# Gated DeltaNet scan: decays and write strengths spread over the partitions by DMA instead of by products with ones

## The chip, the cores and the metric

The program runs on one core of one Trainium2 chip. The metric is the device time of one execution in microseconds (us); lower is better. Engines are named as in the profile: PE is TensorE (PEld its weight loads), DVE VectorE, ACT ScalarE, POOL GpSimd, SP SyncE, which here only issues DMAs.

## What is computed

Two layers of a hybrid diffusion backbone over 1024 latent and 256 context tokens, width 1024, all in float32. Layer 0 has a bidirectional gated DeltaNet of 4 heads, then a mixture of experts (MoE); layer 1 has windowed attention, then an MoE. The change lies in the DeltaNet scan alone. For each direction, head and chunk of tokens the reference has

```
g = jnp.cumsum(to_chunks(log_a), axis=-1)
decay = jnp.exp(jnp.where(incl, g[..., :, None] - g[..., None, :], -jnp.inf))
a_mat = jnp.where(strict, jnp.einsum('nbhid,nbhjd->nbhij', kb, kc) * decay, 0.0)
t_mat = lax.linalg.triangular_solve(eye + a_mat, ...)
qk = jnp.where(incl, jnp.einsum('nbhid,nbhjd->nbhij', qc, kc) * decay, 0.0)
q_dec = qc * jnp.exp(g)[..., None]
def step(s, inp):
    v_new = uc - wc @ s;  o = qd @ s + qkc @ v_new;  s = s * gl + kd^T @ v_new
```

(the three products of `step` are written shortened). `kb` is k times the write strength beta. The difference g_i - g_j needs g once along the partitions (a column, which the kernel has) and once along the free axis, the same on every partition (a row). So does beta. This "row on every partition" of g and of beta is what the change makes in another way.

## The kernel before

The kernel is a chain of stages; an all-engine barrier stands before each, and each engine has its own hand-written program in a stage. `delta_scan` is one stage. It takes chunks of 128 tokens, so there are NT = 10 steps; in step s direction 0 (forward) works on tile s and direction 1 (backward) on its own tile. Both directions, written d0 and d1 here, are interleaved on every engine, and a [128, 4, 128] buffer holds the four heads. Steps 0 and 1 are unrolled, the other eight run in a loop of two steps a pass (`u` is the parity). State `S` is carried from step to step, so a step's last instructions feed the next step's.

One step, in the order of the work:

- POOL multiplies a triangle by log_a (`GU`, L806) and the identity by beta (`BI`, L807) for d0, then for d1, and signals `rows_in`.
- PE multiplies each with a matrix of ones (L967, L968): bank 0 then holds the row of g on all partitions, bank 1 that of beta. Then `g_rows` is signalled. Behind them in PE's queue are K^T K and K^T Q (L958).
- ACT takes exp of bank 0 (`EG`, L852), DVE subtracts the column of g (`Dc`, L894), clips at 0 (L895), ACT takes exp (L855), POOL masks it with the triangle (`Dm`, L811).
- DVE: `DB` = decay x beta row (L900), `AT` = DB x K^T K (L902), `KQ` = Dm x K^T Q (L904), for d0 and then d1. I call the two instances of a line its d0 and d1 instance.
- PE turns AT (L980), DVE makes T (L907, L908) while POOL makes TT (L815, L817); six merge levels invert (1 + A): on each PE makes P (`heads(bank[d][1], AT[d], T[d])`), DVE `Pm` (L912), PE two products, DVE two subtractions (L923, L925).
- The tail: products with S, R (L928, L930), v_new (L859 on ACT), v_decayed (L933), the output (L938), and the state: POOL scales S (L828), DVE adds the new part (L941). L941 of d1 is the last instruction of DVE in a step.

A step's DMAs (QT, KT, K at L787, V at L791) are issued by SP. QT, KT and K of a step are issued two steps ahead, once the step that used the same buffer is through, V when POOL has used the last one.

## Time and profile before

| | us |
|---|---|
| median of 3 runs | 4178.23 (4165.79 to 4182.88) |
| the profiled execution's own time | 4188.01 |
| its span, first to last instruction | 4186.3 |
| mean granted TensorE clock | 0.884 |

The profile is of one execution. Instructions come with the line of the source, the operation and the tiles; idle time stands in brackets with what ended it. A line in a helper (L958) stands for several calls, which the tiles tell apart. A "x8" run of four float32 head products is eight matmul records, since each product is recorded as two.

### The profile page before, as it was taken

The page shows a single profiled execution, that of the slowest core. Times are in us where ns is not written, and L with a number is a line of the kernel's source. Part 1 is how long each engine was busy: PE and PEld are TensorE (multiplying, and loading weights), DVE is VectorE, ACT ScalarE, POOL GpSimd, SP SyncE. Part 2 cuts the span into 40 slices and gives each one's busy share as a digit, 9 for nine tenths or more (in the row PEclk, how much of TensorE's full clock was granted, in tenths as well). Part 3 has the DMA queues.
Part 4 walks back from the last instruction along what each step waited for, and adds up shares of the span by engine and source line. Part 5 has one row for each costly group of instructions (what it writes and reads, how often), then busy time and mean ns, then how long its engine had stood idle before and what let it go on. Part 6 is the DMA issues. An engine that isn't in the chain of part 4 may idle for free. (4 is left out here: it accounts for less than half of the span.)

```text
span 4186.3 us, 47304 instructions
## 1 busy us (share of the span) xinstructions
PE 3273.4 (78%) x15402; PEld 1783.8 (43%) x15403; DVE 1249.3 (30%) x2289; ACT 643.1 (15%) x1426; POOL 537.9 (13%) x523
## 2 busy tenths in 40 slices
PE   4999997999897857399999846776778737978992
PEld 2554443888885324133333303334555323323330
DVE  3313331555556214111111133114554140101114
ACT  2111211000002001000000012115564010000002
POOL 0000001233322111100000030220111120000002
PEclk8899998999998875699999968888999858999996
DMA  5311101011104035587897752003110227989684
GB/s 210 88 42 50 50 17 63 26 41 41 39 24 198 14 147 178 156 336 291 353 393 292 291 201 98 26 28 120 56 37 11 90 96 295 396 318 381 279 347 166
DMA packets 148528, 657.64 MB, mean 157 GB/s; under 512 B 25184, under 2 KB 62848, under 8 KB 117664
## 3 DMA queue, kind: packets, MB, share of 16 engines
q1 hardware_dynamic: 117888, 530.50, 33.4%
q0 software_dynamic: 20912, 72.13, 4.6%
q10 hardware_dynamic: 9584, 53.19, 3.1%
q8 instruction: 79, 1.29, 0.1%
q14 instruction: 65, 0.53, 0.0%
HBM read 586.41 MB, written 69.36 MB: 157 GB/s over the span
## 5 line engine op out<-in xcount | busy, mean ns | idle before, releaser
L1518 PE MATMUL bank<-w,xT 128*64 x3392 | 753.7, 603 | 60.1 <-DMA w<-in_moe_w 44.4
L529 PE MATMUL bank<-aT,w 128*128 128x512 f32 (+1 forms) x1344 | 500.2, 535 | 6.7 <-DVE short L688 5.9
L1518 PEld LDWEIGHTS bank<-w,xT 128*64 128x64 f32 x3392 | 250.1, 139 | 524.3 <-issue 518.5
L1538 PE MATMUL bank<-w,hT 128*64 (+1 forms) x1696 | 380.9, 602 | 37.4 <-issue 37.2
L529 PEld LDWEIGHTS bank<-aT,w 128*128 128x128 f32 x1344 | 266.1, 199 | 236.1 <-issue 220.0
L1610 DVE TENSOR_TENSOR h<-h,bank 128x512 f32<-128x512 f32 x53 | 36.5, 688 | 792.8 <-PE bank L1518 792.8
L1538 PEld LDWEIGHTS bank<-w,hT 128*64 128x64 f32 x1696 | 122.3, 138 | 294.8 <-issue 294.8
L1824 PE MATMUL bank<-at_w_in,aT 128*128 128x512 f32 x416 | 192.2, 624 | 3.4 <-PEq L116 3.4
L1494 PE MATMUL bank<-eye,x 128*128 128x128 f32 x440 | 65.5, 294 | 122.1 <-DMA x<-moe_x,idx_block 97.6
L197 PE MATMUL bank<-ada_w,silu_c 128*2 128x512 f32 x384 | 74.1, 879 | 101.9 <-DMA ada_w<-in_ada_w 101.9
L958 PE MATMUL bank<-T,AT 128*128 128x128 f32 x960 | 143.7, 302 | 11.9 <-DVE T L908 11.9
L1467 POOL DMA_INDIRECT x<-moe_x,idx_block x55 | 53.0, 963 | 704.6 <-PE bank L1494 702.8
L958 PEld LDWEIGHTS bank<-T,AT 128*128 128x128 f32 x960 | 129.1, 210 | 23.0 <-DVE T L908 15.9
L2013 PE MATMUL bank<-eye,probs 128*128 128x128 f32 x640 | 102.1, 292 | 42.9 <-ACT probsT L2076 42.6
L1824 PEld LDWEIGHTS bank<-at_w_in,aT 128*128 128x128 f32 x416 | 83.5, 203 | 106.3 <-issue 106.3
L1494 PEld LDWEIGHTS bank<-eye,x 128*128 128x128 f32 x440 | 55.7, 196 | 168.8 <-DMA x<-moe_x,idx_block 100.9
L958 PE MATMUL bank<-TT,A_T_off 128*128 128x128 f32 x960 | 127.6, 277 | 0.0
L958 PEld LDWEIGHTS bank<-TT,A_T_off 128*128 128x128 f32 x960 | 117.8, 193 | 0.8
L1570 ACT ACTIVATE h<-bank 128x512 f32<-128x512 f32 x53 | 31.7, 598 | 534.2 <-PE bank L1518 534.2
L958 PE MATMUL bank<-A_T_off,TT 128*128 128x128 f32 x800 | 111.5, 285 | 0.0
L1118 PE MATMUL bank<-at_w_out,att 128*128 128x512 f32 x256 | 110.1, 592 | 1.7 <-PEq L116 1.7
L1616 DVE COPY hT<-bank 128x512 f32<-128x512 f32 x53 | 36.6, 691 | 248.6 <-PE bank L1500 248.6
(307 smaller groups left out, 4175.6 us busy)
## 6 DMA issues: line engine op xcount, KB each, us to landing
w<-in_moe_w SPq DMA_DIRECT2D x180, 2048.0 KB, 14.7
ada_w<-in_ada_w SPq DMA_DIRECT2D x48, 1024.0 KB, 9.1
moe_y<-y ACTq DMA_DIRECT2D x53, 512.0 KB
w<-in_moe_w ACTq DMA_DIRECT2D x12, 2048.0 KB, 27.3
w<-in_ab_w_in SPq DMA_DIRECT2D x28, 512.0 KB, 3.9
moe_x<-w SPq DMA_DIRECT2D x18, 512.0 KB, 2.6
moe_y<-zero POOLq DMA_DIRECT2D x1, 8192.0 KB, 27.4
at_w_in<-in_at_w_in SPq DMA_DIRECT2D x3, 2048.0 KB
```

Of the source, the lines that this page charges most:

```text
L197: mm = pe.matmul(self.k.bank[self.bank0 + n][self.on(q), :], self.k.silu_c[:, j, :], self.w[:, c % self.ring, q * self.NW:(q + 1) * self.N ...
L529: mm = pe.matmul(k.bank[3 * s + n][:, 0:width], w[j][:, c, :], aT[:, c, at:at + width], start=(c == 0), stop=(c == KC - 1))
L958: mm = pe.matmul(to[:, h, :], lhs[:, h, :], rhs[:, h, :], start=start, stop=stop)
L1118: mm = pe.matmul(k.bank[2 * (n % 2) + half][:], lhs(c, t), w[:, c, half * 512:(half + 1) * 512], start=(c == 0), stop=(c == KC - 1))
L1467: pool.indirect_dma_start(x[:], None, dr["moe_x"], bass.IndirectOffsetOnAxis(ap=one[:, 0:1], axis=0)).then_inc(x_in, 16)
L1494: t = pe.transpose(k.bank[X[c // 4]][:, (c % 4) * P:(c % 4 + 1) * P], x[:, c:D:KC], k.eye[:])
L1518: mm = pe.matmul(k.bank[UP[half]][u * UNIT:(u + 1) * UNIT, :], xT[:, c, u * UNIT:(u + 1) * UNIT], w13[:, r if u else ds(buf[0], 1), half, ...
L1538: mm = pe.matmul(k.bank[Y[half]][u * UNIT:(u + 1) * UNIT, :], hT[:, c, u * UNIT:(u + 1) * UNIT], w2[:, r if u else ds(buf[0], 1), at:at + ...
L1610: nc.vector.tensor_tensor(h[:], h[:], k.bank[UP[1]][:], ALU.mult).then_inc(h_ready, 1)
L1616: nc.vector.tensor_copy(hT[:].rearrange("p c q -> p (c q)"), k.bank[HT][:]).then_inc(hT_ready, 1)
L1824: mm = pe.matmul(k.bank[3 * s + g][:], aT[:, c, t * P:(t + 1) * P], w[:, c, g * 512:(g + 1) * 512], start=(c == 0), stop=(c == KC - 1))
L2013: mm = pe.transpose(k.bank[6 + f % 2][:, at:at + P], pr[m % 2][:, h, c * P:(c + 1) * P], k.eye[:])
```

## The change

- `GU`, `BI` and their products with ones go, and so do the semaphores `rows_in` (POOL to PE) and `g_rows`.
- Once, before the first step: PE turns g and beta (two transposes to 80 x 128), ACT copies them to a buffer `gbT`, SP writes that to a new DRAM tensor `gate_rows`, and waits until it has landed.
- For each step SP issues four more loads, each of one 2 KB row spread over 128 partitions (256 KB written): g and beta for d0 and d1, into `GR` and `BR`, which have two buffers each. They stand ahead of the step's QT, KT and K loads, and in the first step behind the write.
- ACT's exp, DVE's subtraction and DVE's `DB` read `GR` and `BR` in SBUF, where they read PSUM banks before.
- The masked decay is written into `KQ` itself, v_decayed into the buffer of `R`, so two buffers each go; POOL's masking now waits for the last step's output products (`o_ready`).
- PE's waits for `vd_ready` and `vn_copied` move to the first merge product.

```diff
--- before.py
+++ after.py
@@ -721,11 +721,13 @@
         return [[k.sb(f"{name}{d}{u}", [P, NH, P]) for u in R2] for d in R2]
 
     KT, QT, K, V = per_step("KT"), per_step("QT"), per_step("K"), per_dir("V")
-    GU, BI, Dc, EG = per_dir("g_rows_in"), per_dir("b_rows_in"), per_dir("decay"), per_dir("eg_rows")
-    Dm, AT, KQ = per_dir("decay_masked"), per_dir("AT"), per_dir("KQ")
+    GR, BR, Dc, EG = per_step("g_rows"), per_step("b_rows"), per_dir("decay"), per_dir("eg_rows")
+    gbT = k.sb("g_beta_turned", [2 * NH * NT, 2, P])
+    KQ, AT = per_dir("KQ"), per_dir("AT")
     DB = k.sb("decay_beta", [P, NH, P])
     T, TT, Pm, QTd = per_dir("T"), per_dir("TT"), per_dir("A_T_off"), per_dir("QT_decayed")
-    VB, R, VN, VD, S = per_dir("V_beta"), per_dir("R"), per_dir("v_new"), per_dir("v_decayed"), per_dir("S")
+    VB, R, VN, S = per_dir("V_beta"), per_dir("R"), per_dir("v_new"), per_dir("S")
+    VD = R
 
     consts_in, ones_set, state_set, stats = k.sem("consts_in"), k.sem("ones_set"), k.sem("state_set"), k.sem("stats")
     prep_act, prep_pe, prep_order = k.sem("prep_act"), k.sem("prep_pe"), k.sem("prep_order")
@@ -733,9 +735,9 @@
     def sems(name):
         return [k.sem(f"{name}{d}") for d in R2]
 
-    tile_in, rows_in = [[k.sem(f"tile_in{d}{u}") for u in R2] for d in R2], sems("rows_in")
-    v_in = sems("v_in")
-    g_rows, kk_ready, a_turned, p_ready, dt_ready = (sems(n) for n in ("g_rows", "kk_ready", "a_turned", "p_ready", "dt_ready"))
+    tile_in, rows_in = ([[k.sem(f"{n}{d}{u}") for u in R2] for d in R2] for n in ("tile_in", "rows_in"))
+    v_in, gb_turned, gb_copied, gb_stored = sems("v_in"), k.sem("gb_turned"), k.sem("gb_copied"), k.sem("gb_stored")
+    kk_ready, a_turned, p_ready, dt_ready = (sems(n) for n in ("kk_ready", "a_turned", "p_ready", "dt_ready"))
     ks_ready, vn_ready, o_ready, ds_ready = (sems(n) for n in ("ks_ready", "vn_ready", "o_ready", "ds_ready"))
     e_ready, at_ready, kq_ready, t_ready, pm_ready = (sems(n) for n in ("e_ready", "at_ready", "kq_ready", "t_ready", "pm_ready"))
     tt_ready, r_ready, vd_ready, o_added, s_ready = (sems(n) for n in ("tt_ready", "r_ready", "vd_ready", "o_added", "s_ready"))
@@ -777,7 +779,20 @@
         sp.dma_start(alog[:], dr["ab_a_log"].rearrange("a d h -> a (d h)").to_broadcast([P, 2 * NH])).then_inc(consts_in, 16)
         sp.dma_start(dtb[:], dr["ab_dt_bias"].rearrange("a d h -> a (d h)").to_broadcast([P, 2 * NH])).then_inc(consts_in, 16)
 
+        sp.wait_ge(gb_copied, primed(1))
+        sp.dma_start(dr["gate_rows"].rearrange("x t d n -> (t d) x n").rearrange("a x (h n) -> (a h) x n", h=NH),
+                     gbT[:]).then_inc(gb_stored, 16)
+        sp.wait_ge(gb_stored, primed(16))
+
         def body(s, i, u, tiles):
+            for d in R2:
+                if not isinstance(s, int):
+
+                    sp.wait_ge(eg_ready[d], primed(s - 1))
+                    sp.wait_ge(at_ready[d], primed(s - 1))
+                for x, dst in enumerate((GR, BR)):
+                    sp.dma_start(dst[d][u][:].rearrange("p h n -> p (h n)"),
+                                 dr["gate_rows"][x, ds(tiles[d], 1), d, :].to_broadcast([P, W0])).then_inc(rows_in[d][u], 16)
             for d in R2:
                 if not isinstance(s, int):
 
@@ -802,13 +817,9 @@
 
         def body(s, i, u, tiles):
             for d in R2:
-                pool.wait_ge(g_rows[d], primed(s))
-                nc.gpsimd.tensor_tensor(GU[d][:], all_heads(k.tri[:, d, :]), stat(la, tiles[d], d), ALU.mult).then_inc(rows_in[d], 1)
-                nc.gpsimd.tensor_tensor(BI[d][:], all_heads(k.eye[:]), stat(beta, tiles[d], d), ALU.mult).then_inc(rows_in[d], 1)
-            for d in R2:
                 pool.wait_ge(d_ready[d], primed(s + 1))
-                pool.wait_ge(kq_ready[d], primed(s))
-                nc.gpsimd.tensor_tensor(Dm[d][:], Dc[d][:], all_heads(k.tri[:, d, :]), ALU.mult).then_inc(dm_ready[d], 1)
+                pool.wait_ge(o_ready[d], primed(s))
+                nc.gpsimd.tensor_tensor(KQ[d][:], Dc[d][:], all_heads(k.tri[:, d, :]), ALU.mult).then_inc(dm_ready[d], 1)
             for d in R2:
                 pool.wait_ge(at_ready[d], primed(s + 1))
                 pool.wait_ge(vn_ready[d], primed(s))
@@ -844,12 +855,14 @@
         nc.scalar.activation(kdec[:], kdec[:], ACT.Exp).then_inc(prep_act, 1)
         nc.scalar.activation(egl[:], tot[:], ACT.Exp).then_inc(prep_act, 1)
         nc.scalar.activation(tmp[:], g[:], ACT.Exp).then_inc(prep_act, 1)
+        act.wait_ge(gb_turned, primed(1))
+        nc.scalar.copy(gbT[:], flat[1][0][0:2 * NH * NT, 0:2 * P].rearrange("p (x n) -> p x n", x=2)).then_inc(gb_copied, 1)
 
         def body(s, i, u, tiles):
             for d in R2:
-                act.wait_ge(g_rows[d], primed(s + 1))
+                act.wait_ge(rows_in[d][u], primed((i + 1) * 32))
                 act.wait_ge(qtd_ready[d], primed(s))
-                nc.scalar.activation(EG[d][:], bank[d][0], ACT.Exp).then_inc(eg_ready[d], 1)
+                nc.scalar.activation(EG[d][:], GR[d][u][:], ACT.Exp).then_inc(eg_ready[d], 1)
             for d in R2:
                 act.wait_ge(e_ready[d], primed(s + 1))
                 nc.scalar.activation(Dc[d][:], Dc[d][:], ACT.Exp).then_inc(d_ready[d], 1)
@@ -889,19 +902,19 @@
             for d in R2:
 
 
-                dve.wait_ge(eg_ready[d], primed(s + 1))
+                dve.wait_ge(rows_in[d][u], primed((i + 1) * 32))
                 dve.wait_ge(dm_ready[d], primed(s))
-                st.link(nc.vector.tensor_tensor(Dc[d][:], bank[d][0], stat(g, tiles[d], d), ALU.subtract))
+                st.link(nc.vector.tensor_tensor(Dc[d][:], GR[d][u][:], stat(g, tiles[d], d), ALU.subtract))
                 nc.vector.tensor_scalar(Dc[d][:], Dc[d][:], 0.0, None, ALU.min).then_inc(e_ready[d], 1)
             for d in R2:
                 dve.wait_ge(d_ready[d], primed(s + 1))
 
                 dve.wait_ge(at_ready[1 - d], primed(s + d))
-                st.link(nc.vector.tensor_tensor(DB[:], Dc[d][:], bank[d][1], ALU.mult))
+                st.link(nc.vector.tensor_tensor(DB[:], Dc[d][:], BR[d][u][:], ALU.mult))
                 dve.wait_ge(kk_ready[d], primed(s + 1))
                 nc.vector.tensor_tensor(AT[d][:], DB[:], bank[d][2], ALU.mult).then_inc(at_ready[d], 1)
                 dve.wait_ge(dm_ready[d], primed(s + 1))
-                nc.vector.tensor_tensor(KQ[d][:], Dm[d][:], bank[d][3], ALU.mult).then_inc(kq_ready[d], 1)
+                nc.vector.tensor_tensor(KQ[d][:], KQ[d][:], bank[d][3], ALU.mult).then_inc(kq_ready[d], 1)
             for d in R2:
                 dve.wait_ge(a_turned[d], primed(s + 1))
                 st.link(nc.vector.tensor_tensor(T[d][:], bank[d][0], all_heads(merge[:, d, 0, :]), ALU.mult))
@@ -950,6 +963,12 @@
             pe.matmul(flat[0][d][:, 0:NT * NH], k.tri[:, d, :], la[:, :, NH * d:NH * d + NH], start=True, stop=True)
         pe.matmul(flat[0][2][:, 0:2 * NT * NH], ones[:], la[:].rearrange("p t h -> p (t h)"),
                   start=True, stop=True).then_inc(prep_pe, 1)
+        pe.wait_ge(prep_order, primed(5))
+        pe.wait_ge(prep_act, primed(4))
+        for x, rows in enumerate((g, beta)):
+            turn = pe.transpose(flat[1][0][0:2 * NH * NT, x * P:(x + 1) * P], rows[:].rearrange("p t h -> p (t h)"), k.eye[:])
+        turn.then_inc(gb_turned, 1)
+        pe.wait_ge(gb_copied, primed(1))
         pe.wait_ge(stats, primed(1))
         pe.wait_ge(state_set, primed(3))
 
@@ -959,14 +978,6 @@
             return mm
 
         def body(s, i, u, tiles):
-            for d in R2:
-                pe.wait_ge(rows_in[d], primed(2 * s + 2))
-                pe.wait_ge(r_ready[d], primed(s))
-                pe.wait_ge(vd_ready[d], primed(s))
-                pe.wait_ge(vn_copied[d], primed(s))
-                pe.matmul(flat[d][0][:], ones[:], GU[d][:].rearrange("p h n -> p (h n)"), start=True, stop=True)
-                pe.matmul(flat[d][1][:], ones[:], BI[d][:].rearrange("p h n -> p (h n)"), start=True,
-                          stop=True).then_inc(g_rows[d], 1)
             for d in R2:
                 pe.wait_ge(tile_in[d][u], primed((i + 1) * 48))
                 pe.wait_ge(o_added[d], primed(s))
@@ -975,13 +986,15 @@
                 heads(bank[d][3], KT[d][u], QT[d][u]).then_inc(kk_ready[d], 1)
             for d in R2:
                 pe.wait_ge(at_ready[d], primed(s + 1))
-                pe.wait_ge(eg_ready[d], primed(s + 1))
+                pe.wait_ge(r_ready[d], primed(s))
                 for h in range(NH):
                     mm = pe.transpose(bank[d][0][:, h, :], AT[d][:, h, :], k.eye[:])
                 mm.then_inc(a_turned[d], 1)
             for n in range(MERGES):
                 for d in R2:
                     if n == 0:
+                        pe.wait_ge(vd_ready[d], primed(s))
+                        pe.wait_ge(vn_copied[d], primed(s))
                         pe.wait_ge(t_ready[d], primed(s + 1))
                     else:
                         pe.wait_ge(tt_ready[d], primed(s * MERGES + n))
@@ -2242,6 +2255,7 @@
     for name, shape, dt in (
         ("mods", (2, 2, MODS * D), F32),
         ("heads", (4, NT, P, W0), F32),
+        ("gate_rows", (2, NT, 2, W0), F32),
         ("moe_x", (TOK, D), F32),
         ("att_q", (LT, P, ATT_H // 2 * P), F32),
         ("att_k", (NT + 2, P, ATT_KV * P), F32),
```

DVE's program at the head of the loop-free first step, from the d1 subtraction on; `decay_137` and the like are Dc of d1, `bank` is PSUM. Before:

```order
L894 TENSOR_TENSOR decay_137<-bank,g 128x512
L895 TENSOR_SCALAR decay_137<-decay_137 128x512
L900 TENSOR_TENSOR decay_beta<-decay_136,bank 128x512
L902 TENSOR_TENSOR AT_142<-decay_beta,bank 128x512
L904 TENSOR_TENSOR KQ_144<-decay_masked_140,bank 128x512
L900 TENSOR_TENSOR decay_beta<-decay_137,bank 128x512
```

The same place after:

```order
L907 TENSOR_TENSOR decay_141<-g_rows_134,g 128x512
L908 TENSOR_SCALAR decay_141<-decay_141 128x512
L913 TENSOR_TENSOR decay_beta<-decay_140,b_rows_136 128x512
L915 TENSOR_TENSOR AT_147<-decay_beta,bank 128x512
L917 TENSOR_TENSOR KQ_145<-KQ_145,bank 128x512
L913 TENSOR_TENSOR decay_beta<-decay_141,b_rows_138 128x512
```

The order on DVE is the same; the subtraction and the product `decay_beta` now have both inputs in SBUF.

POOL's program at the head of the first step, before:

```order
L806 TENSOR_TENSOR g_rows_in_132<-tri,log_a 128x512
L807 TENSOR_TENSOR b_rows_in_134<-eye,beta 128x512
L806 TENSOR_TENSOR g_rows_in_133<-tri,log_a 128x512
L807 TENSOR_TENSOR b_rows_in_135<-eye,beta 128x512
L811 TENSOR_TENSOR decay_masked_140<-decay_136,tri 128x512
L811 TENSOR_TENSOR decay_masked_141<-decay_137,tri 128x512
L815 TENSOR_TENSOR TT_149<-AT_142,merge 128x512
L817 TENSOR_TENSOR TT_149<-eye,TT_149 128x512
```

After:

```order
L822 TENSOR_TENSOR KQ_145<-decay_140,tri 128x512
L822 TENSOR_TENSOR KQ_146<-decay_141,tri 128x512
L826 TENSOR_TENSOR TT_152<-AT_147,merge 128x512
L828 TENSOR_TENSOR TT_152<-eye,TT_152 128x512
```

POOL's step now begins with the masking; four instructions ahead of it are gone.

PE's program, from the statistics to the first turn of AT, before:

```order
L951 MATMUL bank<-log_a,ones 128x80
L967 MATMUL bank<-g_rows_in_132,ones 128x512
L968 MATMUL bank<-b_rows_in_134,ones 128x512
L967 MATMUL bank<-g_rows_in_133,ones 128x512
L968 MATMUL bank<-b_rows_in_135,ones 128x512
L958 MATMUL bank<-KT_118 128x128 x4
L958 MATMUL bank<-QT_122,KT_118 128x128 x4
```

After:

```order
L964 MATMUL bank<-log_a,ones 128x80
L969 MATMUL bank<-eye,g 80x128
L969 MATMUL bank<-eye,beta 80x128
L977 MATMUL bank<-KT_118 128x128 x4
L977 MATMUL bank<-QT_122,KT_118 128x128 x4
```

K^T K is now the first thing that PE does in a step; the two turns stand once ahead of the first.

## Rows read from the trace of the kernel before

**Rows 1.** Windows over the scan's steps: busy us (instructions) of PE, PEld, DVE, ACT, POOL.

```profile
722.00:1305.00 583.00, 526.58 (x4000) 481.61 (x4000) 330.42 (x580) 35.17 (x60) 188.52 (x160) 0.95 0.10 31
```

**Rows 2.** Waits in the scan: who waited for whom, us in total, times, longest.

```profile
ACT eg_rows L852 <- PE bank L968: 95.5, 20, 8.9
...
DVE decay L894 <- ACT eg_rows L852: 45.3, 20, 6.9
```

**Rows 3.** Timeline, a step's end and the next one's start: start, duration, instruction.

```profile
957.46 0.68 DVE L941 TENSOR_TENSOR S<-S,bank 128x512 f32<-128x512 f32 x1
...
958.77 1.10 PE L967 MATMUL bank<-g_rows_in,ones 128*128 128x512 f32 x2 [1.66 <-POOL b_rows_in L807]
...
959.48 1.05 POOL L807 TENSOR_TENSOR b_rows_in<-eye,beta 128x512 f32<-128x512 f32 x1
...
961.67 0.69 DVE L894 TENSOR_TENSOR decay<-bank,g 128x512 f32<-128x512 f32 x1 [3.53 <-ACT eg_rows L852]
...
962.40 0.43 DVE L895 TENSOR_SCALAR decay<-decay 128x512 f32<-128x512 f32 x1
...
963.10 0.62 ACT L855 ACTIVATE decay<-decay 128x512 f32<-128x512 f32 x1
...
963.79 1.27 POOL L811 TENSOR_TENSOR decay_masked<-decay,tri 128x512 f32<-128x512 f32 x1 [3.27 <-ACT decay L855]
...
964.11 1.24 DVE L895 TENSOR_SCALAR decay<-decay 128x512 f32<-128x512 f32 x1
...
965.27 0.67 DVE L900 TENSOR_TENSOR decay_beta<-decay,bank 128x512 f32<-128x512 f32 x1
...
965.98 0.69 DVE L902 TENSOR_TENSOR AT<-decay_beta,bank 128x512 f32<-128x512 f32 x1
...
967.18 0.68 DVE L900 TENSOR_TENSOR decay_beta<-decay,bank 128x512 f32<-128x512 f32 x1
```

**Rows 4.** The same timeline, where DVE makes T and POOL makes TT.

```profile
968.67 1.27 POOL L817 TENSOR_TENSOR TT<-eye,TT 128x512 f32<-128x512 f32 x1
...
969.81 0.69 DVE L908 TENSOR_TENSOR T<-eye,T 128x512 f32<-128x512 f32 x1
969.89 1.74 POOL L815 TENSOR_TENSOR TT<-AT,merge 128x512 f32<-128x512 f32 x1
...
971.14 1.04 DVE L908 TENSOR_TENSOR T<-eye,T 128x512 f32<-128x512 f32 x1
971.71 1.61 POOL L817 TENSOR_TENSOR TT<-eye,TT 128x512 f32<-128x512 f32 x1
```

**Rows 5.** The same timeline, products P of two merge levels on PE.

```profile
970.56 3.78 PE L958 MATMUL bank<-T,AT 128*128 128x128 f32 x16 [0.95 <-DVE T L908]
...
978.43 2.17 PE L958 MATMUL bank<-T,AT 128*128 128x128 f32 x16
```

**Rows 6.** Windows, three steps from L941 of d1 to the next; PEclk is third from the end.

```profile
957.50:1015.50 58.00, 52.74 (x400) 48.48 (x400) 32.97 (x59) 3.52 (x6) 18.81 (x17) 0.94 0.12 37
1073.60:1130.40 56.80, 50.15 (x400) 46.06 (x400) 32.95 (x60) 3.52 (x6) 18.87 (x18) 1.00 0.13 38
1244.80:1304.20 59.40, 53.38 (x400) 48.91 (x400) 32.98 (x60) 3.52 (x6) 17.96 (x16) 0.94 0.00 1
```

**Rows 7.** Timeline, the start of the scan.

```profile
720.19 0.24 DVE L879 COPY g_total<-bank 128x80 f32<-128x80 f32 x1
...
728.53 0.69 DVE L894 TENSOR_TENSOR decay<-bank,g 128x512 f32<-128x512 f32 x1 [6.86 <-ACT eg_rows L852]
...
734.03 0.69 DVE L902 TENSOR_TENSOR AT<-decay_beta,bank 128x512 f32<-128x512 f32 x1
```

**Rows 8.** DMA issues in the steps, us to landing at the end.

```profile
V<-heads SPq DMA_DIRECT2D x18, 256.0 KB, 2.6
...
K<-heads SPq DMA_DIRECT2D x16, 256.0 KB, 4.2
```

**Rows 9.** DMA issues of the whole program: one row spread over 128 partitions.

```profile
norm_rows<-in_norm_final SPq DMA_DIRECT2D x1, 512.0 KB, 7.5
```

## The prediction, made blind

> **What bounds the kernel now.** I read the windows first: the ten steps of the scan take 583 us, 14% of the span, and no engine is busy all the time: PE 527, DVE 330, POOL 189 [rows 1]. Barriers stand around the stage, so what it gains comes off the end one for one, and nothing outside it changes. Next the waits inside it. DVE waited 45.3 us ahead of its subtraction L894 for ACT's exp, and ACT waited for PE's products with ones [rows 2]. Then the timeline of one step's start, to see who is last. DVE ends the old step with L941 at 957.46 and is idle until 961.67. POOL's fourth product (L807) runs until 960.53, PE's products follow their POOL inputs from 958.77, ACT's exp comes between PE and DVE. So the chain POOL, PE, ACT, DVE stands bare between two steps, and K^T K, which PE has behind it, comes out in time for L902. The product AT, on which all the rest of a step hangs, starts at 965.98, 8.52 us after L941 [rows 3]. This boundary speaks for all: of the 45.3 us of idle some 8 belong to the scan's first wait (6.86 for d0 [rows 7] and a little for d1), which leaves about 4.1 for each of the nine boundaries, here 3.53 and a little for d1.
>
> **What the change does to a boundary.** The four POOL products (1.04 each), the PE products and the wait for ACT go. The row loads of step s+1 stand in SP's queue right behind the V loads of step s, and those go out in step s-1, when POOL has used V. So the rows have more than a whole step, 58 us [rows 6], and land in 3 to 8 [rows 8, 9]: hidden, and the tile loads behind them wait for the end of step s-1 anyway. ACT's EG has its data early, and runs behind v_new. POOL's new wait for `o_ready` was already met by its own scaling of S. PE does K^T K and K^T Q right behind the old step's last product. A set of four head products takes 1.1 at full clock (two take 2.17 [rows 5]), so d0's two sets are done about 2 us after L941's start and d1's about 4, before AT wants them.
>
> I now lay the new start out from L941's start as zero, with distances from the trace. An instruction that need not wait starts 0.08 before the end of the one ahead (L900 after L895), a chained one 0.73 or 0.71 after its start [rows 3]. L894 at 0.60, L895 at 1.33 (0.43 long), L894 of d1 1.68, L895 of d1 2.41; ACT's exp of d0 1.79 to 2.41, POOL's masking from 2.48, L900 at 2.75, AT at 3.46. That would save 8.52 - 3.46 = 5.1.
>
> **But DVE and POOL hinder each other**, and this is the term that I take most care of. L895 of d1 took 1.24, not 0.43: POOL's masking had begun 0.32 before it and ended at 965.06 [rows 3]. L908 of d1 took 1.04, not 0.69, beside L815, and POOL's L815 and L817 took 1.74 and 1.61 where 1.27 is usual [rows 3, 4]. All of it fits one rule of exclusion: the later one gets in 0.14 before the end of the earlier, in order of arrival, and an engine that already waits comes ahead of the other's next. L900, with one input in PSUM, did not hinder or wait. After the change L900 has both inputs in SBUF, as L908 has.
>
> The page "SBUF — State Buffer" of the Trainium skill (section "Who interferes with whom") says just that: a DVE instruction with two SBUF inputs contends with one of GpSimd that reads SBUF, and one with a single SBUF input does not. By this rule the change makes two instructions for each direction contend that did not. The trace agrees for L908; no row shows L900 in its new form.
>
> With exclusion I lay it out again. L895 of d1 has the port from 2.41 to 2.70, so masking ends at 3.97, L900 gets in at 3.83 and ends at 4.51, AT starts at 4.54. Masking of d1 then ends at 5.64; L815 of d0 arrives at 5.60 and L900 of d1 at 5.74 (1.20 after AT, as in rows 3 and therefore later than POOL), so it waits until 6.73. From there DVE and POOL hold each other up at each turn, and L908 of d1 ends 7.46 after AT, not 6.20 as before (972.18 - 965.98) [rows 3, 4]. Saved: 8.52 - 4.54 - 1.26 = 2.7. If instead masking gets in 0.08 before L895 of d1, which is as near as it looks, L895 ends at 4.04, AT starts at 4.67, L900 of d1 comes ahead of L815, and L908 ends only 0.4 late: saved 3.85 - 0.4 = 3.4. I cannot tell which from these rows; I take the middle, 3.1, nine times: 28.
>
> **TensorE's clock.** Of nine steps one ran at full clock and took 56.8; most show 0.94 and take 58.0, the last 59.4 [rows 6]. The low level (1.2 GHz) sets in while PE has little but the turns of AT to do, between AT at 965.98 [rows 3] and the first P at 970.56, and that P then takes 3.78 for a pair, not 2.17 [rows 5]. The change makes this sparse stretch longer, from some 4.6 us to 6.4 (K^T Q done at 4, P at 4.54 + 4.58 + 1.26 = 10.4), so I expect the low level in every step. The cost in a step is bounded by the rows: 1.2 us, up to 2.6. It is already paid in most steps, so I put no net change, with -1 to +1.5 a step as bounds.
>
> **The small terms.** The loop's branch and DVE's address work at a step's start were covered by the idle time and now are not: 0.1 to 0.3 for every second step, in all 1 us. First step: g is ready at 720.43 and DVE starts at 728.53 [rows 7]. Now there are two turns (0.9: a quarter of a set of four in the slow P each [rows 5]), a copy by ACT of half the width of its 0.62 exp [rows 3] (0.4), the issue and landing of the write (3 to 4; loads land in 2.6 to 4.2 [rows 8], the write is shorter), then four row loads, 0.5 apart by my estimate, with 2.6 to 4.2 to land: d0's rows come at about 727.5, d1's at 729. The QT, KT and K loads, issued before the preparation until now, stand behind them. If each load takes some 0.7 us of transfer (estimated from K's landing 1.6 later than V's as the last of several [rows 8]), the tiles of d0 are in at 731 and of d1 at 733. PE starts K^T K cold, so AT of d0 comes at about 735 instead of 734.03, of d1 2 us late. PE, once busy, is then at full clock sooner. I take +1, with 0 to +6: a spread row took 7.5 to land elsewhere [rows 9], though behind other traffic.
>
> **Sum.** 9 x 3.1 = 28, less 1, less 1 or so for the start: 26 to 27 off the profiled execution's 4188.0, which gives 4161. That execution stands 10 us above the median shown, so against the median 4178.2 - 27 = 4151.
>
> **The rivals.**
> - *The exclusion holds for L908 but not for L900 in its new form.* For it: no row shows it. Then AT starts at 3.46, and POOL is some 0.4 late for T: 4.6 a boundary, 41 in all, less 2: 4139. Chance 0.2.
> - *POOL wins each exchange*, so that L900 of d0 waits for both maskings: AT at 5.77 and about 1 late at T, 1.8 a boundary, 16 less 2: 4164. Against it: L908 of d0 got in between two POOL instructions at 969.8 [rows 4]. Chance 0.18.
> - *Slower: the clock stays low through a merge level more.* PE is the bound there: a level is P and two products of the same size for each direction, three times 2.17 less their overlap, say 5.5 us at full clock. A further level at 1.2 GHz costs up to as much again in each step, 49 in all, against 27 gained: 4200. It turns the sign at half a level, some 3 us a step. For it: a longer sparse stretch at each boundary. Against it: PE is busy without a gap from the first P on, and by the next level's P, 7.9 us on, the clock was back [rows 5]. The page "TensorE: Matmul & The Clock Gate" (Part 1) has the clock back after sustained work, which speaks against it too. Chance 0.05.
> - *Rows or tiles late.* In the steps that would need a landing of over 58 us. In the first it costs 5 to 10 once: 4158. Chance 0.07.
> - The forecast itself: 0.5.
>
> **How the numbers follow.** 0.5%, about what a measurement of this kernel can tell from no change, is 21 us. The forecast's own spread is 20 to 33 saved, the clock included, of which a small part lies under 21; the ports' first rival and the late first step lie beyond or near. That gives 0.69 faster, 0.27 same (most of "POOL wins" and the forecast's lower edge), 0.04 slower. The range runs from the first rival (4133, with a kinder clock) to a little beyond the second (4170).
>
> **What would show it.** In the new trace: no products with ones; DVE busy from L941 into the subtraction without a gap; AT of d0 4.5 to 4.7 us after L941's start (3.5: no exclusion for L900; 5.8: POOL wins); `decay_beta` longer than 0.68, at about 1.7; the step 54.5 to 55.3 us, not 58; a low clock of 5 to 7 us in each step; the first AT at 735 to 736. I am wrong if a step is above 56 us, if DVE waits for `rows_in` after the first step, or if the start of the scan moves by over 6 us.

## The result, and the profile after

The changed kernel took 4149.03 us (median of 5 executions, 4138.61 to 4152.57), the kernel before on the same chip 4178.23 (median of 5, 4165.79 to 4186.01). The ratio is 0.9929, with an interval of 0.9903 to 0.9955: 19 to 41 us less. The profiled execution took 4152.57, its span is 4150.9, and the mean granted clock 0.882 stands beside 0.884 before.

The boundary of [rows 3] in the timeline after (us from the start of the span, duration, engine, line, operation, and in brackets the idle time before it and what ended it). The last addition to S, L941 before, is L954 now, L894 is L907, L895 is L908, L900 is L913, L902 is L915:

```profile
953.66 1.13 PE L977 MATMUL bank<-KT 128*128 128x128 f32 x8
...
954.03 0.68 DVE L954 TENSOR_TENSOR S<-S,bank 128x512 f32<-128x512 f32 x1
...
954.63 0.68 DVE L907 TENSOR_TENSOR decay<-g_rows,g 128x512 f32<-128x512 f32 x1
...
955.35 0.43 DVE L908 TENSOR_SCALAR decay<-decay 128x512 f32<-128x512 f32 x1
...
955.69 0.68 DVE L907 TENSOR_TENSOR decay<-g_rows,g 128x512 f32<-128x512 f32 x1
...
956.41 0.43 DVE L908 TENSOR_SCALAR decay<-decay 128x512 f32<-128x512 f32 x1
...
956.60 3.04 POOL L822 TENSOR_TENSOR KQ<-decay,tri 128x512 f32<-128x512 f32 x2 [3.50 <-ACT decay L868]
956.75 1.75 DVE L913 TENSOR_TENSOR decay_beta<-decay,b_rows 128x512 f32<-128x512 f32 x1
...
958.54 0.69 DVE L915 TENSOR_TENSOR AT<-decay_beta,bank 128x512 f32<-128x512 f32 x1
...
959.60 1.26 POOL L826 TENSOR_TENSOR TT<-AT,merge 128x512 f32<-128x512 f32 x1
959.74 1.67 DVE L913 TENSOR_TENSOR decay_beta<-decay,b_rows 128x512 f32<-128x512 f32 x1
960.94 1.60 POOL L828 TENSOR_TENSOR TT<-eye,TT 128x512 f32<-128x512 f32 x1
...
963.36 0.95 DVE L921 TENSOR_TENSOR T<-eye,T 128x512 f32<-128x512 f32 x1
963.85 1.60 POOL L828 TENSOR_TENSOR TT<-eye,TT 128x512 f32<-128x512 f32 x1
...
964.46 2.26 PE L977 MATMUL bank<-T,AT 128*128 128x128 f32 x9 [1.16 <-DVE T L921]
964.95 1.05 DVE L921 TENSOR_TENSOR T<-eye,T 128x512 f32<-128x512 f32 x1
```

DVE goes from L954 into the subtraction without a gap, and PE is at K^T K by then. AT of d0 starts at 958.54, 4.51 us after L954 (before: 8.52). `decay_beta`, the product that was L900, takes 1.75 and 1.67 beside POOL's KQ and TT, where it took 0.67 and 0.68. The last `T<-eye,T` of d1 starts at 964.95 and ends at 966.00, 7.46 after AT (before: 6.20). Over all twenty of `decay_beta`, in the view of groups (the two of the first step, 0.69 and 1.39, are in the mean; the other eighteen take 1.66 to 1.77):

```profile
L913 DVE TENSOR_TENSOR decay_beta<-decay,b_rows 128x512 f32<-128x512 f32 x20 | 32.9, 1644 | 0.0
```

The windows of two steps and of the whole scan, the counterpart of [rows 1, 6] (stretch, length, busy PE, PEld, DVE, ACT, POOL with instructions, granted clock, DMA share, GB/s):

```profile
954.03:1008.69 54.66, 48.57 (x394) 46.47 (x394) 34.37 (x59) 3.49 (x6) 15.68 (x12) 0.94 0.18 58
1172.58:1227.19 54.61, 48.52 (x394) 46.42 (x394) 34.35 (x59) 3.48 (x6) 15.67 (x12) 0.94 0.12 38
722.00:1283.00 561.00, 487.71 (x3924) 466.13 (x3923) 343.47 (x585) 35.90 (x64) 157.07 (x120) 0.93 0.18 57
```

All nine steps take 54.6 to 54.8 us, against 58.05 as the usual step before, and each holds 6.8 us at the low clock (1.2 GHz). POOL has 12 operations in a step where it had 16.

The stretch after the scan, which the change does not touch, first before and then after:

```profile
1304.90:4186.30 2881.40, 2143.47 (x9620) 964.41 (x9620) 711.63 (x1520) 473.40 (x1163) 317.63 (x324) 0.87 0.52 203
```

```profile
1282.50:4150.90 2868.40, 2140.88 (x9620) 958.80 (x9620) 711.58 (x1520) 474.16 (x1163) 318.43 (x324) 0.87 0.52 204
```

The counts are equal and the stretch is 13.0 us shorter. That is how one execution differs from another: in the twelve traces of this document the same untouched stretch takes from 2854.9 us (e8) to 2881.4 (before), in no order that the changes explain, and the five executions of the kernel before lie 20 us apart. So single times that differ by 20 us say little. What the change did is read inside the scan, from the end of the copy of `g_total` to the end of the last addition to S, and the experiments are compared by the same length:

| kernel | scan, us | usual step | AT after last addition to S | decay_beta, d0 |
|---|---|---|---|---|
| before | 584.4 | 58.05 | 8.5 | 0.68 |
| after | 559.4 | 54.65 | 4.52 | 1.75 |
| e1 masking late | 554.5 | 54.4 | 3.45 | 0.69 |
| e2 only g by DMA | 547.2 | 52.0 to 55.0 | 3.7, every other 4.3 to 4.8 | 0.68 |
| e3 only beta by DMA | 577.8 | 55.9 to 58.3 | 5.8 to 6.1, every other 7.3 to 7.7 | 1.76 |
| e4 tiles first | 555.8 | 54.7 | 4.52 | 1.75 |
| e5 filler | 549.4 | 53.65 | 4.52 | 1.75 |
| e6 = e1 + e4 + e5 | 534.6 | 52.3 | 3.45 | 0.69 |
| e7 beta folded into K | 534.2 | 50.05, three 56.5 to 56.9 | 2.72, long steps 7.4 to 8.2 | none |
| e8 rows alone | 555.7 | 54.7 | 4.52 | 1.75 |
| e9 = e7, loads later | 530.7 | 50.05, three 54 to 56.3 | 2.72, long steps 5.3 to 7.2 | none |
| e10 = e7, more filler | 520.6 | 50.45, two 51.4 | 2.72 | none |

### The profile page after: what moved, and what is told of

It reads as the page before. It is cut to its first block and busy times, and to the rows that moved or that the text cites. A ratio compares the mean times of both kernels' runs of the same rounds, so it can differ in the third digit from the quotient of the medians.

```text
span 4150.9 us, 47198 instructions
## 1 busy us (share of the span) xinstructions
PE 3232.5 (78%) x15324; PEld 1763.2 (42%) x15325; DVE 1261.4 (30%) x2289; ACT 644.2 (16%) x1427; POOL 507.0 (12%) x483
## 5 line engine op out<-in xcount | busy, mean ns | idle before, releaser
L1590 ACT COPY xT<-bank 128x512 f32<-128x512 f32 x55 | 32.3, 587 | 493.2 <-PE bank L1531 331.2
```

## The experiments

**e1: is it the port?** POOL's masking is moved behind its V_beta, so that no POOL instruction stands beside DVE before AT.

```diff
-                pool.wait_ge(o_ready[d], primed(s))
-                nc.gpsimd.tensor_tensor(KQ[d][:], Dc[d][:], all_heads(k.tri[:, d, :]), ALU.mult).then_inc(dm_ready[d], 1)
...
+                pool.wait_ge(kq_ready[d], primed(s + 1))
+                nc.gpsimd.tensor_tensor(KQ[d][:], KQ[d][:], all_heads(k.tri[:, d, :]), ALU.mult).then_inc(dm_ready[d], 1)
...
-                nc.vector.tensor_tensor(KQ[d][:], KQ[d][:], bank[d][3], ALU.mult).then_inc(kq_ready[d], 1)
+                nc.vector.tensor_tensor(KQ[d][:], Dc[d][:], bank[d][3], ALU.mult).then_inc(kq_ready[d], 1)
```

> Changed kernel, but POOL's masking of KQ moves from the step's start to behind V_beta (DVE multiplies the unmasked decay with K^T Q, POOL masks the product later). Theory, the shared ports: the product decay_beta takes 1.66 to 1.77 us only because POOL holds the way into SBUF; without the masking d0's takes 0.69 and AT starts 3.5 us after the last L941-like add of the step before (4.5 in the changed kernel); d1's still waits for POOL's first TT product; T of d1 ends 7.1 after AT (7.45 now), so a step takes 53.2 us instead of 54.6. Rival, the row in SBUF is slow to read or DVE waits for something else: decay_beta stays at 1.7 and AT at 4.5. Second rival, the rhythm of TensorE's clock sets the step: AT moves as said and the step stays at 54.6.

The timeline of DVE at the same boundary:

```profile
950.42 0.68 DVE L953 TENSOR_TENSOR S<-S,bank 128x512 f32<-128x512 f32 x1
951.02 0.69 DVE L906 TENSOR_TENSOR decay<-g_rows,g 128x512 f32<-128x512 f32 x1
...
953.15 0.69 DVE L912 TENSOR_TENSOR decay_beta<-decay,b_rows 128x512 f32<-128x512 f32 x1
953.87 0.69 DVE L914 TENSOR_TENSOR AT<-decay_beta,bank 128x512 f32<-128x512 f32 x1
```

With POOL away `decay_beta` of d0 takes 0.69, its value before, and AT comes 3.45 us after the addition to S: 3.46 was laid out in the prediction for "no exclusion". That of d1, which still meets POOL's first TT product, takes 1.38 to 1.47. So the new form with two SBUF inputs is slow only beside POOL, and the exclusion is the reason. But of the 1.3 us that T comes earlier the step kept 0.5, and 53.2 us a step had been expected. Two windows say why:

```profile
949.50:1004.10 54.60, 49.32 (x395) 47.38 (x394) 33.10 (x59) 3.48 (x6) 15.11 (x12) 0.94 0.19 58
1004.10:1057.10 53.00, 47.79 (x395) 45.85 (x394) 33.08 (x59) 3.50 (x6) 15.15 (x13) 0.97 0.19 59
```

Eight steps took 53.8 to 54.6 with 6.8 us of low clock, and the one that had 3.4 us of it (mean 0.97) took 52.94. PE comes to the sparse stretch earlier and leaves it earlier, and the time of the low clock now falls on its products. The first product behind the first pair of P shows it, before, after and in e1:

```profile
974.13 1.78 PE L958 MATMUL bank<-A_T_off,TT 128*128 128x128 f32 x8
```

```profile
968.01 1.08 PE L977 MATMUL bank<-A_T_off,TT 128*128 128x128 f32 x8
```

```profile
963.13 1.92 PE L976 MATMUL bank<-A_T_off,TT 128*128 128x128 f32 x8
```

At full clock it takes 1.06. The low stretch ends 5.1 us after the start of the first P before (at 975.7), 3.6 after (968.0) and 6.1 in e1 (965.7). This can be priced. From the end of T of d1 to the next addition to S a step takes 41.7 us at full clock, whatever the kernel (41.71 in the one such step before, 41.72 in e5, e6 and e7). In a usual step it takes 43.3 before, 42.7 after and 43.9 in e1, so the low clock costs 1.6, 1.0 and 2.2 us. Why the low stretch falls where it does in each kernel no run here settles.

e1 took 4136.51 us, beside 4185.31 for the kernel before, one execution each.

**e2 and e3: one half of the change each.** In e2 g comes by DMA, and beta again by POOL's product with the unit matrix and PE's product with ones, just ahead of K^T K; in e3 it is the other way around.

```diff
+                pool.wait_ge(b_rows[d], primed(s))
+                nc.gpsimd.tensor_tensor(BI[d][:], all_heads(k.eye[:]), stat(beta, tiles[d], d), ALU.mult).then_inc(bi_in[d], 1)
...
-                st.link(nc.vector.tensor_tensor(DB[:], Dc[d][:], BR[d][u][:], ALU.mult))
+                st.link(nc.vector.tensor_tensor(DB[:], Dc[d][:], bank[d][1], ALU.mult))
...
+                pe.matmul(flat[d][1][:], ones[:], BI[d][:].rearrange("p h n -> p (h n)"), start=True,
+                          stop=True).then_inc(b_rows[d], 1)
```

> Changed kernel, but beta alone goes back to POOL's product with the identity and PE's product with ones, for each direction just ahead of its K^T K; g still comes by DMA. The product decay_beta has one input in PSUM again. Theory, ports: decay_beta takes 0.68 for both directions although POOL masks beside it, AT starts at 3.8 us, T of d1 ends some 1.7 us earlier than in the changed kernel, step 52.9 to 53.5 us, so half of the change undone is better than the whole. Rival, the POOL and PE work put back stands in the way: AT at 5 or later and a step of 55 to 56 us.

> The other half undone: g by POOL's product with the triangle and PE's product with ones, beta by DMA. Theory: the chain POOL, PE, ACT, DVE is back on the path, shorter than before the change since POOL makes two products and not four: subtraction 2.1 us after the last add of the step before, AT at 6.0 (8.5 before the change, 4.5 after), step 56.1 us. decay_beta stays long at 1.3 to 1.8. Rival, that POOL's four products and not the chain of engines were the cost: AT below 5 us and a step below 55.

The twenty of `decay_beta` in e2 (from what to what, least, median and most in ns), and the boundary in e3:

```profile
L919 DVE TENSOR_TENSOR decay_beta<-decay,bank x20: 679/681/689, 733.5 to 1222.0; 128x512 f32<-128x512 f32 x20
```

```profile
953.15 0.68 DVE L960 TENSOR_TENSOR S<-S,bank 128x512 f32<-128x512 f32 x1
...
956.87 0.69 DVE L912 TENSOR_TENSOR decay<-bank,g 128x512 f32<-128x512 f32 x1 [3.04 <-ACT eg_rows L870]
...
959.00 1.76 DVE L919 TENSOR_TENSOR decay_beta<-decay,b_rows 128x512 f32<-128x512 f32 x1
...
960.80 0.69 DVE L921 TENSOR_TENSOR AT<-decay_beta,bank 128x512 f32<-128x512 f32 x1
```

In e2 one input is in PSUM, and with the masking just where it stands in the changed kernel none of the twenty is longer than 0.69. In e3 the chain POOL, PE, ACT is back: DVE waits 3.04 us for ACT, and `decay_beta` is at 1.76 as well. The scan is 12.2 us shorter than in the changed kernel in e2 and 18.4 longer in e3. Against the kernel before, g alone by DMA brings 37.2 us, beta alone 6.6, and both together 25.0. So the gain comes from g, which stands at the head of the chain, and once g is there the DMA for beta costs more than it brings. Of the 12.2 us between e2 and the changed kernel, 1.6 lie in the first step, where two rows fewer are loaded. In the other nine T ends 1.2 us earlier on average, and what follows T takes as long in both (42.8 and 42.7), though the low clock in e2 is 3.4 us or none in a step. That the products with ones, which PE has again in the sparse stretch, keep the low clock short is likely, not shown. 4133.23 and 4163.30 us, beside 4185.31, one execution each. Both have steps of uneven length (neighbours differ by 0.7 to 3.0 us), which the changed kernel has not; e7 to e10 come back to that. Of e3's expected numbers AT (6.0) came, but the subtraction starts 3.7 us after the addition to S and not 2.1, and the step is 57.1 on average and not 56.1.

**e4 and e8: the start of the scan.** e4 issues the first step's QT, KT and K ahead of the write of the rows. e8 also holds the first V and all later loads back until the first rows have landed.

```diff
+        for d in R2:
+            load_tiles(0, (0, CT - 1), d)
         sp.wait_ge(gb_copied, primed(1))
...
+                if isinstance(s, int) and s == 0:
+                    for e in R2:
+                        sp.wait_ge(rows_in[e][0], primed(32))
```

> Changed kernel, but the first step's QT, KT and K loads are issued ahead of the write of the turned rows, as before the change. Theory, the first step lost 3.1 us because its row loads and tile loads shared the DMA engines and stood behind the write: first rows land 5.5 to 6.5 us after g_total is copied (9.3 in the changed kernel), first AT 10 to 11 us after it (16.7 now, 13.6 before the change), the scan 5 to 6 us shorter. Rival, a row spread over 128 partitions is slow in itself: rows still land 8 to 9 us after the copy and the gain is 3 us or less. The other steps as they are, 54.6.

> Changed kernel with the first tiles ahead of the write, and SP holding back all later loads until the first step's four row loads have landed. d0's two rows landed 8.8 us after the copy of g_total with V and the next step's rows behind them. Theory, the DMA engines were shared: alone, the second row of d0 lands 3 to 4 us after its issue (5.5 before) and the first AT comes 2 us earlier. Rival, a row that 128 partitions read from one 2 KB place is slow in itself: 5 us or more from issue to landing, and the first AT at 12 to 12.6 us after the copy as before.

The start in the changed kernel, in e4 and in e8:

```profile
724.30 0.35 SPq L783 DMA_DIRECT2D gate_rows<-g_beta_turned  x1
...
726.37 0.43 SPq L794 DMA_DIRECT2D b_rows<-gate_rows  x1
...
732.42 0.69 DVE L907 TENSOR_TENSOR decay<-g_rows,g 128x512 f32<-128x512 f32 x1 [8.06 <-DMA b_rows<-gate_rows]
...
736.16 2.04 PE L977 MATMUL bank<-KT 128*128 128x128 f32 x8 [12.34 <-DMA K<-heads]
...
739.81 0.69 DVE L915 TENSOR_TENSOR AT<-decay_beta,bank 128x512 f32<-128x512 f32 x1 [4.15 <-PE bank L977]
```

```profile
722.54 0.43 SPq L801 DMA_DIRECT2D b_rows<-gate_rows  x1
...
728.08 0.69 DVE L913 TENSOR_TENSOR decay<-g_rows,g 128x512 f32<-128x512 f32 x1 [7.55 <-DMA b_rows<-gate_rows]
...
731.86 0.69 DVE L921 TENSOR_TENSOR AT<-decay_beta,bank 128x512 f32<-128x512 f32 x1
```

```profile
726.05 0.43 SPq L801 DMA_DIRECT2D b_rows<-gate_rows  x1
...
730.81 0.69 DVE L916 TENSOR_TENSOR decay<-g_rows,g 128x512 f32<-128x512 f32 x1 [6.76 <-DMA b_rows<-gate_rows]
...
733.96 0.69 DVE L924 TENSOR_TENSOR AT<-decay_beta,bank 128x512 f32<-128x512 f32 x1
```

In the changed kernel the write lands within 1.7 us, but the subtraction starts 6.05 us after the issue of the second row of d0, and K^T K waits till 736.16 for tiles behind them. With the tiles first AT comes 12.6 us after the copy of `g_total` and not 16.7. With no loads but the first step's own four rows in flight a spread row still takes 4.75 us (d0) and 5.06 (d1: issued 727.00, landed 732.06), and AT comes at 11.2. So both theories hold in part. In e4 the rows landed 8.8 us after the copy, as the rival said, but 3.6 us were won; in e8 the other loads turn out to be worth 0.8 us of d0's landing and 1.4 at AT, not 2, and most of the time stays with the rows themselves. How long a single row would take alone no run shows. The scan as a whole won 3.6 us in e4 and 3.7 in e8: what e8 gained at its first AT was lost again behind T of the first steps (43.1 us from T to the next addition to S in its second step, 42.8 in e4's), with no wait for a DMA there, which points to where the low clock falls and not to its later loads. 4142.36 beside 4185.31 (one execution each), and 4135.14 (one execution) beside 4169.12 (median of 8).

**e5 and e6: the clock.** e5 puts products that nobody reads (K^T K into the free bank[d][1]) ahead of and behind the turns of AT, to keep PE busy: one set of four, two, and one. PE's waits for `vd_ready` and `vn_copied` move ahead of them. e6 joins e1, e4 and e5.

```diff
+            heads(bank[1][1], KT[1][u], KT[1][u])
...
                 mm.then_inc(a_turned[d], 1)
+                for _ in range(2 - d):
+                    heads(bank[d][1], KT[d][u], KT[d][u])
```

> Changed kernel, with products that nobody reads put into PE's sparse stretch at each step's start (K^T K again, into the bank that the first merge product then overwrites: one set of four before AT is turned, two after the turn of d0, one after that of d1). Theory: the changed kernel's step is AT at 4.5, T 7.45 after it, and a low-clock stretch of 6.8 us that costs 1.2 us; with the filler the clock stays at 2.4 GHz, the first pair of P takes 2.2 and not 3.7 us, and a step takes 53.4 us, though PE has more to do. Rival, the low clock lies in time that nobody waits for: granted clock 1.00 and still 54.6 a step.

> Changed kernel with the late masking, the first tiles ahead of the write, and the filler products. Theory: the late masking brought AT and T forward by 1.3 us and the step by only 0.5, since the low clock set in earlier and took it back; with the filler the whole 1.3 shows: 52.1 us a step, 22 us off the scan, 4 more from the first step, some 26 us under the changed kernel and 55 under the one before. Rival, PE's own work bounds the merge levels and the filler delays the turn of AT: 53 us a step or more.

A step of e5:

```profile
949.80:1003.50 53.70, 50.27 (x426) 48.21 (x426) 34.29 (x60) 3.48 (x6) 15.68 (x12) 1.00 0.18 59
```

There are 16 more products (32 records), and the step is 1.0 us shorter, at full clock throughout; AT and T come where they were. So the low clock cost each step 1.0 us. e5 took 4135.53, one execution, beside 4169.12 (median of 8). e6 took 4125.49 (median of 4, 4119.63 to 4135.49), ratio 0.989 with an interval of 0.9852 to 0.9928. Its steps are 52.24 to 52.42, 2.3 less than after. Masking late and filler apart brought 0.5 and 1.0, together 2.3: the 0.8 of e1 that the clock had taken is there once the clock stays up.

**e7, e9 and e10: beta without a product on DVE.** The product KT x beta rows goes to POOL, in place in the row buffer and a step ahead; PE then forms K^T K with it, and AT = decay x bank. With e1, e4 and one set of filler behind each turn. e9 changes only when the tile loads go out; e10 only puts back e5's full filler. (The last step makes a scaled KT for each direction that nobody uses.)

```diff
+                nc.gpsimd.tensor_tensor(BR[d][u][:], KT[d][u][:], BR[d][u][:], ALU.mult).then_inc(kb_ready[d], 1)
...
-                heads(bank[d][2], KT[d][u], KT[d][u])
+                pe.wait_ge(kb_ready[d], primed(s + 1))
+                heads(bank[d][2], KT[d][u], BR[d][u])
...
-                st.link(nc.vector.tensor_tensor(DB[:], Dc[d][:], BR[d][u][:], ALU.mult))
...
-                nc.vector.tensor_tensor(AT[d][:], DB[:], bank[d][2], ALU.mult).then_inc(at_ready[d], 1)
+                nc.vector.tensor_tensor(AT[d][:], Dc[d][:], bank[d][2], ALU.mult).then_inc(at_ready[d], 1)
```

> As the last one, but the product decay_beta goes from DVE altogether: POOL multiplies K^T by the spread row of beta in the middle of the step before, where it idles, in place in the row's buffer, and PE takes that as one input of K^T K; the filler is one set after each turn. At the last step POOL does one such product for nothing. Theory, DVE and its hold-ups with POOL are what stands between two steps: AT at 2.8, the second at 4.0, T of d1 ends at 8.4 after the last add instead of 10.7; a step takes 50 us, if the clock stays up. Rival, the clock falls with the smaller filler: 51 to 52 us.

AT comes 2.72 us after the addition to S, T of d1 ends at 8.3, and six steps take 50.0 to 50.1 at full clock, so the smaller filler is enough for them. But three take 56.5 to 56.9. There, at the head of each later pass of the loop, PE stands still in the middle of K^T K, and its records name no one who releases it ("issue"):

```profile
938.19 0.93 PE L991 MATMUL bank<-b_rows,KT 128*128 128x128 f32 x6 [2.00 <-issue]
941.53 0.59 PE L991 MATMUL bank<-b_rows,KT 128*128 128x128 f32 x2 [2.42 <-issue]
```

The same stretch of time (790 to 1250 us) in the view of the DMA queues, queue by queue: packets, MB, share. First before, then after, then e7:

```profile
q8 instruction: 34, 0.56, 0.5%
```

```profile
q8 instruction: 9, 0.15, 0.1%
```

```profile
q8 instruction: 36, 0.59, 0.5%
```

The queue that fetches instructions moved 34 packets before, 9 after and 36 in e7. The difference lies behind the loop's first pass: between 940 and 1235 us it moved 24 packets before and 24 in e7, and none after. I took the standstill for a fetch that has to stand behind the tile loads, and moved these in e9:

```diff
-                    sp.wait_ge(ds_ready[d], primed(s - 1))
+                    sp.wait_ge(kk_ready[1], primed(s))
```

> e7_beta_in_k with one wait of SP changed: the QT, KT and K loads of a step are issued not at the end of the step before the last, but when the K^T K of the last one are done, some 4 us later. e7 had steps of 50.05 us, but three of them took 56.5 to 56.9: at the head of each pass of the loop PE stood still in the middle of K^T K, for 2.0 and 2.4 us that no wait explains, while the DMA engines moved the new tiles, and the clock then fell. Theory, PE waits for its own instructions, whose fetch queues behind the tile loads: with the loads later the fetch is quick and all steps take 50.1 us, the scan 20 us less than in e7. Rival, the fetch at the loop's head is slow whatever the DMA engines do: the same three steps stay at 53 us or more. The first step's rows aren't touched.

> e7_beta_in_k with the filler of e5_filler (two more sets of four products a step on PE). e9 showed that the standstill at the loop's head doesn't come from the tile loads. The traces differ in another number: kernels whose loop stands still or may do so fetched instructions 34 to 37 times between 790 and 1250 us (before, e2, e3, e7, e9), the others 9 or 10 times, e5 and e6 with more PE instructions than e7 among them. Theory one, what decides is where the loop's instructions happen to lie: with two sets more the fetches may fall to 10 and the steps are even, 50.5 to 51 us, some 20 us under e6. Theory two, the loop of e7 is too long for what PE holds: it gets worse, still 36 fetches or more and three long steps.

```profile
937.98 0.93 PE L991 MATMUL bank<-b_rows,KT 128*128 128x128 f32 x6 [2.37 <-issue]
940.75 0.59 PE L991 MATMUL bank<-b_rows,KT 128*128 128x128 f32 x2 [1.84 <-issue]
```

```profile
986.50:1037.90 51.40, 49.57 (x425) 48.03 (x425) 31.58 (x57) 3.51 (x6) 17.39 (x14) 1.00 0.20 61
```

In e9 the two standstills shown are 2.37 and 1.84 us where they were 2.00 and 2.42, with no tile load beside them: between 935 and 941 us the DMA queues moved two instruction packets and nothing else. So the tile loads are not the cause, though they add to it: over the three heads the two standstills together are 4.4 to 4.8 us in e7 and 3.4 to 4.2 in e9. In e10, which has more PE instructions than e7, the packets are 9, no step is over 51.4, and none has low clock. So the number of products does not decide. (In its two steps of 51.4 POOL's TT and DVE's T of d1 come to the port at the same moment, 994.40 in the one shown, and POOL has it first: T takes 1.80 and not 0.69. The scan is 14 us shorter than e6's, where 20 were expected.) e2 (35), e3 (34), e7 (36) and e9 (37) stand still at the loop's later heads, once (1.6 to 2.2 us) in e2 and e3 and twice in e7 and e9, and their fetches go on through all passes. After, e1, e4, e6, e8, e10 (9 each) and e5 (10) have no standstill, and all their packets come before 940 us. The kernel before moved 34 as well and has no standstill in its records. That its wait for POOL at a step's start hides the fetches is argued, not shown; at one loop's head, 1073.57, PE's first product comes 1.79 us after L941 where it comes at 1.31 at 957.46, which would fit. What makes the loop's instructions be fetched again in one kernel and not in the other, I can't tell from these runs; where its code lies is a guess.

e7 took 4132.82 (median of 5, 4129.97 to 4146.98), ratio 0.9907, interval 0.9877 to 0.9938; e9 4138.32 (median of 5), ratio 0.991, interval 0.9892 to 0.9927. By their times neither can be told from the changed kernel or from each other, although their scans are 25 and 29 us shorter than its scan. e10 took 4112.29 (median of 4, 4108.13 to 4116.66) beside 4176.33, ratio 0.9844 with an interval of 0.9827 to 0.986. That is 58 to 72 us less than before, and the interval lies wholly below the changed kernel's.

## Why the prediction was right

4151 was predicted and 4149.03 measured, inside the range and on the likeliest side, faster. The mechanism is right: the bare chain is gone, and AT comes where the layout with exclusion has it. That the numbers meet to 2 us is in part luck, as the steps show:

- **AT 4.54 after the addition to S; decay_beta at about 1.7.** Measured 4.51 to 4.52 and, behind the first step, 1.66 to 1.77. The exclusion holds for L900 in its new form. e1 and e2 show the reason from both sides: POOL away (d0 in e1), or one input in PSUM (e2), and it is 0.69 or less again. The rival "not for L900" is refuted, "POOL wins each exchange" as well (AT would be at 5.8). The rule of the Trainium skill that the prediction weighed ("SBUF — State Buffer", "Who interferes with whom") agrees with these runs: 1.75 us beside POOL with two inputs in SBUF, 0.68 with one.
- **T.** Of the two orders that I could not tell apart, in which masking or L895 of d1 has the port first, it is L908 (L895 before): it starts at 956.41, 0.43 long, and masking at 956.60. That gave T 7.46 after AT and 2.7 saved; measured 7.45 and 2.75. I had taken the middle, 3.1.
- **3.1 a step, 28 in all.** Measured 3.2 (57.86 less 54.66 as means of nine), 28.8 in all. The sum is right, but from other parts, and that is luck. As means of nine, T of d1 ends 14.74 us after the addition to S before and 11.96 after: 2.8 of the 3.2, where the middle of the two orders had 3.1. The way from there to the next addition takes 43.12 before and 42.70 after. These other 0.4 are the clock's, for which the prediction had put nothing.
- **The low clock in every step, with no net change.** It is in every step, 6.8 us, as before in six of nine. The rival in which it stays a merge level longer did not occur. But there is a net change, in favour, and the cost was read too small. In a usual step the low clock cost 1.6 us before and 1.0 now, since it ends 3.6 and not 5.1 us behind the start of the first P (under e1); e5, where it is gone, confirms the 1.0. The 1.2 of the prediction is 58.0 less the 56.8 of the full-clock step, but in that step AT came 0.35 later than in the usual one, 8.87 us after L941 and not 8.52, which hid a part:

```profile
1073.57 0.68 DVE L941 TENSOR_TENSOR S<-S,bank 128x512 f32<-128x512 f32 x1
...
1082.44 0.69 DVE L902 TENSOR_TENSOR AT<-decay_beta,bank 128x512 f32<-128x512 f32 x1
```

- **The loop's branch, 1 us in all.** Not there: the nine steps lie within 0.16 us.
- **The start, +1 with 0 to +6.** The first AT is 3.1 later, and the first step's end 3.75. The step that was too small is "d0's rows come at about 727.5", which was by loads of ordinary tiles with 2.6 to 4.2 us; they took 6 from the issue, and 4.75 with only the four rows in flight. The tiles behind them then held K^T K back (4.15 of AT's wait). [rows 9] had pointed that way.
- **Sum.** 26 to 27 predicted, 25.1 in the scan (28.8 less 3.75). The 29.2 between the medians and the 35.4 between the two profiled spans also hold what differs from execution to execution; the scan began 2.7 later in the second, and the rest after it was 13.0 shorter. That the medians lie 4 us further apart than the scan explains is well inside their interval.

## What to carry to other kernels

When a chain over four engines stands bare between two iterations, ask which of its inputs comes first: g alone was worth more than the whole change (37.2 against 25.0 us of the scan), and moving beta's rows from PSUM to SBUF put DVE's product into contention with POOL. Lay such a boundary out on paper with the port held by one at a time, in order of arrival; AT came out to within 0.03 us, and T for one of the two orders that were open. Measure a step in two parts, up to the last T and from there: the second part is 41.7 us at full clock in every kernel but e10 (41.9), so what it has above that is the clock's price. Then ask what clock the time gained will be spent at: e1 gave T 1.3 us and the step 0.5, and only with PE kept busy did it get the rest.

## What was not expected of the hardware

- A row of 2 KB spread over 128 partitions lands 4.75 to 5.1 us after its issue with three more such rows in flight, and 5.5 to 6 with other loads, where a tile of 256 KB, the same bytes written, takes 2.6 to 4.2 among its neighbours [rows 8].
- Products that nobody reads shorten a step by 1.0 us, by holding the clock at 2.4 GHz (e5).
- PE can stand still twice, for 1.6 to 3.1 us each, in the middle of a row of products at a loop's head, in kernels whose instruction queue goes on moving packets behind the loop's first pass (34 to 37 against 9 or 10 in 460 us). e7's long steps cost 6.4 to 6.8 us each, more than the two standstills together (4.4 to 4.8), and their clock is low for 6.8 us; the one long step of e9 at full clock cost 3.9, with standstills of 3.4.
